# Moving the product keys behind the query blocks, and eleven of sixteen top-16 searches of each dense tile with them

## What is computed

```python
q = (tokens @ w_query).reshape(Ntok, PEER_HEADS, 2, PEER_DK)          # 8 heads x 2 halves x 128
s = jnp.einsum('nhpd,hpkd->nhpk', q, sub_keys)                        # 128 scores a list, 16 lists a token
s_top, i_top = lax.top_k(s, K)                                        # the 16 largest of each list
cand = (s_top[:, :, 0, :, None] + s_top[:, :, 1, None, :]).reshape(Ntok, PEER_HEADS, K * K)
best, pos = lax.top_k(cand, K)                                        # 16 experts a head
gate = jax.nn.softmax(best, axis=-1)
...
a = jax.nn.gelu(einsum('nd,nhkd->nhk', xb, expert_down[idx]));  y = einsum('nhk,nhkd->nd', gate * a, expert_up[idx])
```

## Time and profile before

| | |
|---|---|
| median of three runs | 1619.63 us |
| profiled execution, its own time | 1619.37 us |
| its span in the profile | 1617.6 us |
| PE busy | 1597.2 us (99%) |
| DVE busy | 1140.9 us (71%) |
| ACT busy | 665.7 us (41%) |
| POOL busy | 820.0 us (51%) |
| DMA, mean over the span | 263 GB/s |

### The profile page before, as it was taken

How to read it: one execution, slowest core, us unless ns; L and a number is a source line. 1 busy time by engine, 2 the same in 40 slices (tenths; PEclk the granted TensorE clock), 3 DMA queues, 4 the chain that set the end, 5 groups by cost and what they waited for, 6 DMA issues and landing times.

```text
span 1617.6 us, 25384 instructions
## 1 busy us (share of the span) xinstructions
PE 1597.2 (99%) x9227; PEld 1423.1 (88%) x9227; DVE 1140.9 (71%) x2214; ACT 665.7 (41%) x995; POOL 820.0 (51%) x523
## 2 busy tenths in 40 slices
PE   8999999999999999999999999999999999999998
PEld 6888888888889999999999999998888888888886
DVE  4155451351509999997999997339888888888887
ACT  5352442441534344434444544443333333333333
POOL 4463276423244989996877777856222222222220
PEclk9999999999999999999999999999999999999999
DMA  5332243313434999997999999949999999999992
GB/s 196 92 103 71 76 150 96 104 53 118 151 97 136 348 338 337 333 349 236 330 407 400 400 412 402 357 145 398 396 337 348 333 350 334 350 335 347 340 330 77
DMA packets 154442, 424.96 MB, mean 263 GB/s; under 512 B 15728, under 2 KB 65904, under 8 KB 154224
## 3 DMA queue, kind: packets, MB, share of 16 engines
q1 hardware_dynamic: 89088, 229.41, 41.5%
q0 software_dynamic: 41472, 151.01, 25.2%
q10 hardware_dynamic: 23792, 43.33, 7.0%
HBM read 379.88 MB, written 43.25 MB: 262 GB/s over the span
## 4 chain that ended last, share of the span: by engine, by line
PE 90%; DVE 4%; ACT 2%; POOL 2%; DMA 1%; issue 1%; DVEq 0%; SPq 0%; ACTq 0%
PE psum L1459 28%; PE psum L1461 27%; PE psum L1460 27%; PE psum L1748 4%; POOL w_low L457 1%; DMA hid_dram<-arena 1%; PE psum L1695 1%; ACT kept L547 1%; POOL arena L486 1%; DVE arena L1069 0%; ACT w_high L577 0%; PE psum L1582 0%; DMA kept<-x_in 0%; DVE hT_low L1041 0%; PE psum L1431 0%
## 5 line engine op out<-in xcount | busy, mean ns | idle before, releaser
L457 POOL TENSOR_TENSOR w_low<-kept,w_high 128x1024 fp32r<-128x1024 f32 x212 | 520.1, 2457 | 309.3 <-ACT w_high L577 307.5
L1459 PE MATMUL psum<-hT_high,w_high 128*128 128x352 f32 (+2 forms) x1408 | 483.9, 344 | 6.2 <-POOL w_low L457 6.1
L1461 PE MATMUL psum<-hT_high,w_low 128*128 128x352 f32 (+2 forms) x1408 | 477.1, 339 | 0.0
L1460 PE MATMUL psum<-hT_low,w_high 128*128 128x352 f32 (+2 forms) x1408 | 476.5, 338 | 0.0
L1459 PE MATMUL psum<-up_high,wgt_high 128*128 128x512 f32 x768 | 299.0, 389 | 0.0
L1460 PE MATMUL psum<-up_low,wgt_high 128*128 128x512 f32 x768 | 299.0, 389 | 0.0
L1461 PE MATMUL psum<-up_high,wgt_low 128*128 128x512 f32 x768 | 299.0, 389 | 0.0
L1459 PEld LDWEIGHTS psum<-hT_high,w_high 128*128 128x128 f32 x1408 | 265.3, 188 | 21.6 <-ACT arena L814 3.7
L577 ACT ACTIVATE w_high<-kept 128x1024 fp32r<-128x1024 f32 x212 | 223.7, 1056 | 128.1 <-PE psum L1461 91.2
L1460 PEld LDWEIGHTS psum<-hT_low,w_high 128*128 128x128 f32 x1408 | 265.1, 188 | 12.4 <-issue 0.5
L1461 PEld LDWEIGHTS psum<-hT_high,w_low 128*128 128x128 f32 x1408 | 264.8, 188 | 12.6
(11 more groups left out here) (251 smaller groups left out, 1956.4 us busy)
## 6 DMA issues: line engine op xcount, KB each, us to landing
kept<-down_in SPq DMA_DIRECT2D x128, 512.0 KB, 6.6
arena<-up_in SPq DMA_DIRECT2D x128, 512.0 KB, 5.7
kept<-front_w SPq DMA_DIRECT2D x92, 512.0 KB, 3.6
gate_dram<-arena ACTq DMA_DIRECT2D x40, 512.0 KB, 8.9
hid_dram<-arena ACTq DMA_DIRECT2D x112, 176.0 KB
arena<-hid_dram SPq DMA_DIRECT2D x112, 176.0 KB, 5.1
kept<-gate_dram SPq DMA_DIRECT2D x24, 640.0 KB, 8.3
arena<-gate_dram SPq DMA_DIRECT2D x8, 640.0 KB, 8.8
```

The costliest lines, as they stand in the source:

```text
L457: nc.gpsimd.tensor_tensor(lower, ring[:, p % RING, :], high.bitcast(F32), ALU.subtract).then_inc(low_ready, 1)
L1459: nc.tensor.matmul(out, lhs[0], rhs[0], start=first, stop=False)
L1460: nc.tensor.matmul(out, lhs[0], rhs[1], start=False, stop=False)
L1461: return nc.tensor.matmul(out, lhs[1], rhs[0], start=False, stop=last)
```

## The change

Each query block is followed by the key products of the list of the block before, for all tiles at once (`key_products`), and ACT copies them with one instruction into `score` (`key_out`). Two groups of sparse key products stay in front (`KS` = 2); the last dense products (n = 15) stand behind first product 0. DVE searches sparse list 8 + n as it comes, and behind it the same list of the three dense tiles for n = 0 to 6; list 15 and lists 0 to 2 of the dense tiles (n = 7 to 10, twelve lists) come after the sparse `choose` and its gates. Eleven of sixteen lists of a dense tile are thus searched outside its `choose`, into tiles of their own (`early_top`, `more_top`), and four copies bring them into `dense_k`. Each dense tile has two dots instead of three between the steps of its five other lists, so 18 a tile and `DOTS_A` = 54. `AHEAD` goes from 60 to 48, with all blocks that hang on it; the gathers of rows 5 and 6 move from i = 1 to i = 2, and `DOTS_END` goes from 14 to 26 rows, so that all 160 rows are still fetched.

```diff
-EXP_AT = (16, 32, 52)
-TURN_AT = (20, 40, 60)
+EXP_AT = (14, 26, 41)
+TURN_AT = (18, 33, 48)
...
-FIRST_EDGE = 44
+FIRST_EDGE = 32
...
-DOTS_SCORES = (3, 3, 3, 3)
+DOTS_SCORES = (2, 2, 2, 2)
+EARLY, MORE = 8, 3
...
-DOTS_END = (1,) * 14
+DOTS_END = (1,) * 26
...
-        KS = 4
+        KS = 2
+        KEYS = KS + 16
...
-                if i == FIRST_GATHER + 1:
+                if i == FIRST_GATHER + 2:
                     while k < RING_A:
                         if k == 5:
-                            pool.wait_ge(pk_done, KS + 4 * DT)
+                            pool.wait_ge(pk_done, KEYS)
                         down_row(k)
                         k += 1
-                while k < DOTS_A and i > FIRST_GATHER and (k - RING_A) * (AHEAD - 8 - FIRST_GATHER) < (i - FIRST_GATHER - 1) * (DOTS_A - RING_A):
+                while k < DOTS_A and i > FIRST_GATHER + 1 and (k - RING_A) * (AHEAD - 8 - FIRST_GATHER) < (i - FIRST_GATHER - 1) * (DOTS_A - RING_A):
...
+            def key_out(n):
+                j, tiles = (n + RAW) % 16, NT if n < 16 - RAW else DT
+                act.wait_ge(pk_done, KS + n + 1)
+                nc.scalar.activation(score[:, 0:tiles, j * NK:(j + 1) * NK],
+                                     psum[:, DB[n % 2], 0:tiles * NK].rearrange("p (t k) -> p t k", k=NK), ACT.Copy).then_inc(pk_out, 1)
...
             for n in range(16):
                 query_out(n)
...
+                if n:
+                    key_out(n - 1)
+                if n == 14:
                     act.wait_ge(best_ready, 1)
                     nc.scalar.activation(sparse_k.ebest, sparse_k.ebest, ACT.Exp).then_inc(e_ready, 1)
...
+            early_at(0)
+            key_out(15)
...
-            choose(score[:, ST, :], sparse_k, 0, (0, 0, 0, 0), (0, 0, 0, 0), 0, sparse_k.hk, 0, (2, KS))
...
+            dve.wait_ge(pk_out, KS)
+            top16(lists_of(ST, [place(sparse_k, j) for j in range(RAW)]), 0, none)
+            for n in range(EARLY):
+                dve.wait_ge(pk_out, KS + n + 1)
+                top16(lists_of(ST, [place(sparse_k, RAW + n)]) + (early_lists(n) if n < EARLY - 1 else []), 0, none)
+            choose(sparse_k, 0, none, 0, sparse_k.hk, 0)
             nc.vector.scalar_tensor_tensor(idx3.bitcast(U32), sparse_k.hk[:, 0, :], float(NK), sparse_k.hk[:, 1, :],
                                            ALU.mult, ALU.add).then_inc(idx_ready, 1)
             step(gates_of(sparse_k, gate3, 1))
+            for n in range(EARLY - 1, EARLY + MORE):
+                dve.wait_ge(pk_out, KS + n + 1)
+                top16(early_lists(n), 0, none)
...
             for n, t in enumerate(CHOSEN):
-                kd = choose(score[:, t, :], dense_k, kd, DOTS_SCORES, DOTS_CAND, DOTS_HOT, hk if n else hk_last, max(n - 1, 0))
+                for to, early, more in ((dense_k.top, early_top[t], more_top[t]),
+                                        (dense_k.topi.bitcast(U32), early_topi[t].bitcast(U32), more_topi[t].bitcast(U32))):
+                    step.put(nc.vector.tensor_copy(to[:, RAW:RAW + EARLY, :], early))
+                    step.put(nc.vector.tensor_copy(to[:, 0:MORE, :], more))
+                kd = top16(lists_of(t, [place(dense_k, j) for j in range(MORE, RAW)]), kd, DOTS_SCORES)
+                kd = choose(dense_k, kd, DOTS_CAND, DOTS_HOT, hk if n else hk_last, max(n - 1, 0))
...
             for n in range(16):
                 if n >= 4:
                     pe.wait_ge(qp_out, n - 3)
                 columns(68 + n, hT_half, SEQ if n < 16 - RAW else DN, 4 + n % 4)
...
+                if n:
+                    key_products(n - 1)
...
             for i in range(AHEAD):
+                if i == 1:
+                    key_products(15)
```

More of the change, by code:

```diff
@@ L212, in build @@
         hk = dense_k.hk
+        early_top, early_topi = ([at(kb + j, EARLY * TK, EARLY, TK) for kb in (205.5, 206.5, 99)] for j in (0, 0.5))
+        more_top, more_topi = ([at(92 + 0.375 * t + j, MORE * TK, MORE, TK) for t in range(DT)] for j in (0, 0.1875))
         esum = at(27.75, 16)
@@ L793, in _ @@
                 query_out(n)
-                if n == 8:
-                    sparse_key_out(2)
-                    sparse_key_out(3)
-            for c in range(4 * DT):
-                if c == 8:
-                    high(USED + 2)
-                act.wait_ge(pk_done, KS + c + 1)
-                g = KEY_ORDER[c // DT]
-                nc.scalar.activation(score[:, c % DT, g * 512:(g + 1) * 512], psum[:, PB[c], :], ACT.Copy)\
-                    .then_inc(pk_out, 1)
-                if c == 3:
+                if n:
+                    key_out(n - 1)
+                if n == 14:
                     act.wait_ge(best_ready, 1)
                     nc.scalar.activation(sparse_k.ebest, sparse_k.ebest, ACT.Exp).then_inc(e_ready, 1)
+            high(USED + 2)
             def early_at(i):
@@ L820, in early_tiles @@
                     early_at(i)
-            for i in range(4):
+            early_at(0)
+            key_out(15)
+            for i in range(1, 4):
                 early_at(i)
@@ L1193, in top16, with lists_of, choose @@
                 return k
-            def choose(scores, u, k, between_scores, between_cand, between_hot, hk, hk_free, copied=(None,)):
-                for part, groups in enumerate(copied):
-                    if groups is not None:
-                        dve.wait_ge(pk_out, groups)
-                    each = 16 // len(copied)
-                    k = top16([(scores[:, j * NK:(j + 1) * NK], u.top[:, j, :], u.topi[:, j, :].bitcast(U32))
-                               for j in range(part * each, (part + 1) * each)], k, between_scores)
+            def lists_of(t, places):
+                return [(score[:, t, j * NK:(j + 1) * NK], top, topi.bitcast(U32)) for j, top, topi in places]
+            def choose(u, k, between_cand, between_hot, hk, hk_free):
                 pairs = u.pairs.bitcast(BF16).rearrange("p (a r) -> p a r", r=2)
@@ L1263, in _, with place, early_lists @@
             step(nc.vector.tensor_copy(psum[:, 3, 0:P], at(205.5, P)))
-            choose(score[:, ST, :], sparse_k, 0, (0, 0, 0, 0), (0, 0, 0, 0), 0, sparse_k.hk, 0, (2, KS))
+            none = (0, 0, 0, 0)
+            def place(u, j):
+                return j, u.top[:, j, :], u.topi[:, j, :]
+            def early_lists(n):
+                j = (n + RAW) % 16
+                return [pair for t in range(DT) for pair in lists_of(
+                    t, [(j, early_top[t][:, n, :], early_topi[t][:, n, :]) if n < EARLY else
+                        (j, more_top[t][:, n - EARLY, :], more_topi[t][:, n - EARLY, :])])]
+            dve.wait_ge(pk_out, KS)
[4 more added lines that the diff above has]
+            choose(sparse_k, 0, none, 0, sparse_k.hk, 0)
             nc.vector.scalar_tensor_tensor(idx3.bitcast(U32), sparse_k.hk[:, 0, :], float(NK), sparse_k.hk[:, 1, :],
@@ L1716, in _, with key_products @@
             pe.wait_ge(ffns.high, 2)
+            def key_products(n):
+                j, bank = (n + RAW) % 16, DB[n % 2]
+                pe.wait_ge(qp_out, n + 1)
+                pe.wait_ge(pk_out, KS + n - 1 if n >= 2 else 1)
+                for t in range(NT if n < 16 - RAW else DT):
+                    ins = nc.tensor.matmul(psum[:, bank, t * NK:(t + 1) * NK],
+                                           qpT_s[:, j, :] if t == ST else qpT[:, j, t * P:(t + 1) * P],
+                                           keysT[:, j, :], start=True, stop=True)
+                ins.then_inc(pk_done, 1)
             for n in range(16):
@@ L1720, in _ @@
                 columns(68 + n, hT_half, SEQ if n < 16 - RAW else DN, 4 + n % 4)
-                if n == 8:
-                    pe.wait_ge(qp_out, 8)
-                    sparse_keys(2)
-                    pe.wait_ge(pk_out, 1)
-                    sparse_keys(3)
-            pe.wait_ge(pk_out, KS)
-            for c in range(4 * DT):
-                g, t = KEY_ORDER[c // DT], c % DT
-                pe.wait_ge(qp_out, max(c // DT * 4 + 4, {4: 13, 5: 14}.get(PB[c], 0)))
-                if c >= 4:
-                    pe.wait_ge(pk_out, KS + (c - 1 if c >= 10 else c - 3))
-                for hp in range(4 * g, 4 * g + 4):
-                    ins = nc.tensor.matmul(psum[:, PB[c], hp % 4 * NK:(hp % 4 + 1) * NK], qpT[:, hp, t * P:(t + 1) * P],
-                                           keysT[:, hp, :], start=True, stop=True)
-                ins.then_inc(pk_done, 1)
+                if n:
+                    key_products(n - 1)
             def first_product(i):
```

9 lines of the change are left out of this document (4 added, 5 removed).

## The result

The changed kernel takes **1633.56 us** (median of six runs, 1628.95 to 1638.40), the kernel before 1620.31 beside it. The ratio on record, which is not the quotient of these two medians, is 1.0076, with a 95% interval from 1.0058 to 1.0094. It is slower, by 13 us in the medians and 12.3 us by the ratio. The forecast was 1628.5. The range's upper end, 1633.0, lies 0.6 us under the raw median; the ratio applied to the 1619.63 us that the forecast started from gives 1631.9, inside the range. The profiled execution took 1631.19 us, 11.8 more than the profiled one of before.

The account below looks back on a forecast made before the run. PE was taken to bound the kernel, busy for 1597.2 of 1617.6 us. 1619.37 (profiled) + 7.4 (stall) + 1.5 (clock) = 1628.3, so 1628.5 us against the median; range 1622.5 to 1633.

Parts of the forecast that it names:

- PE, ACT: Up to block 0: PE starts it at 520.1, switching matmul kinds costs nothing, ACT's sparse exponential ends at 516.3.
- DVE to the first dot: DVE behind the exponential: gates, twelve lists of 16.1 us, `h_row`, copies, maxima; first dot done at 538.8, now 526.6.
- DVE had no slack after 481.82: DVE in the kernel before: no slack from the sparse tile's lists at 481.82 to the first dot at 525.44.
- POOL and the stall: At block 3: row 7 waits for its dot, low part ready at 543.5, PE waits 11.1 us, +7.4 us.
- rival A: At block 3: dots are in time, PE waits 0.6 us, time 1616.5 us; chance 0.07.
- C: At block 3: the stall is half, POOL or DVE order hiding some, 1620 to 1625 us; chance 0.09.
- The clock: PE behind the stall: a slow start after idling costs 1.5 us, between 0 and 3.
- Further on: From block 3 on: nothing won back, little lost, 0 to 2 us, taken as 0; last tile in time by 6 us.
- Rival B: Stall, then DVE's last tile misses 715, or ACT waits for best scores at `EXP_AT`: 1633.5 us; chance 0.12.
- The sentence on the copies: DVE's four copies of tiles 2 and 3 can each meet a POOL subtraction, making 0.9 us a tile too little.
- The range: Whole-kernel time: 1622.5 to 1633 us, meant to take in 8 of 10.

Follow-up runs that it names:

- e1: Changed kernel with the twelve searches behind the sparse gates left out, their outputs set to zero: 1626.04 us, ratio 1.0037 to the kernel before.
- e2: Changed kernel with sixty unread matmuls ahead of block 3 to keep PE busy in the stall: 1637.86 us, ratio 1.0104 to the kernel before.
- e6: Changed kernel with the old, longer calendar (gates behind block 59, 66 dots): 1629.02 us, ratio 1.0051 to the kernel before.
- e10: e6 with the sixty unread matmuls ahead of block 3: 1628.52 us, ratio 1.0058 to the kernel before.
- e12: e6 without the twelve searches behind the sparse gates, their outputs set to zero: 1617.80 us, ratio 0.9992 to the kernel before.
- e3: Changed kernel with rows 5 and 6 back behind block 1 instead of block 2: 1636.37 us, ratio 1.0103 to the kernel before.
- e8: e7 with gates behind block 55 instead of 59, 1.18 rows a block instead of 1.08: 1618.38 us, ratio 0.9991 to the kernel before.
- e5: Changed kernel with rows from 7 on started three blocks later and then denser: 1626.62 us, ratio 1.0043 to the kernel before.
- e7: Changed kernel with rows from 7 on three blocks later, gates behind block 59, 60 dots: 1615.62 us, ratio 0.9970 to the kernel before.
- e9: Kernel before, with rows 5 and 6 one block later and rows from 7 on three blocks later: 1620.28 us, ratio 0.9998.

## Why the prediction was right, and where not

- **PE, ACT:** block 0 at 519.98 (forecast 520.1), exponential done at 516.1 (516.3), no cost in changing between kinds of matmul. Right.
- **DVE to the first dot:** gates 516.1 (forecast 516.3), `h_row` at 533.17 (533.3), copies 0.5 us (0.9), first dot done at 538.3 (538.8). The twelve searches took 16.2 us (16.1). Right, and e1 shows that they are the cause. That DVE had no slack after 481.82 overlooks its wait of 1.6 us at 522.32, which changes no term.
- **POOL and the stall:** row 7 at 538.61 (538.9), low part ready at 543.2 (543.5), wait 10.9 us (11.1), +7.2 us (+7.4). Right; rival A and C are out.
- **The clock:** it fell, and cost 2.0 us in the trace (forecast 1.5, bounds 0 and 3). e2 shows that idleness is the cause.
- **"Further on" is the term that was mis-sized.** I set it at 0 with 2 at the most. In the profiled execution it was 2.6 us (11.8 less 9.2), and e6 against the changed kernel says 4 us by their ratios, whose intervals overlap. The time came out inside the range, or at its edge by the raw median, because the stall and the clock, the two terms of the forecast's 8.9 us, were each right to 0.5 us. The step compared POOL's own 3.8 us a block with PE's, and asked only whether DVE's last tile is in time, which it was (711.9, and PE asked at 717.4; forecast 709 and 715). It didn't compare dots with rows, though its own numbers held that: 18 dots in 57.7 us are 1.21 a block of 3.88, and the calendar issues 47 rows in 40 blocks, 1.18. By the trace the tiles took 58.5, 60.4 and 57 us, and the dots lay 3.22 us apart, which is 1.20 a block of 3.86. A row waits for the dot of seven rows before, a low part stands behind the row, and POOL, with 3.8 us of its own in 3.86, wins back little of what it loses at a tile's end. The kernel before had 1.14 rows a block to 1.16 dots: hardly more margin, but its row 7 went out 4.7 us behind its dot, where the changed kernel's went out on it, and no later gather waited. That this lead at the start counts beside the margin is argued from the traces and not tested.
- **Rival B** had the sign but not the place: no turn was missed. The sentence on the copies, by which each could meet a subtraction, came true for one of twelve (2.23 us at 654.56, the others 0.17 to 0.23), so the Trainium skill's sentence ("GPSIMD Engine Reference", Specifications) on the shared way to SBUF, weighed there, gives the direction and not the count. Other short operations met it more often, as the last section shows.
- **The range** had to hold this term's true width. Three of the six runs, 1635.9 to 1638.4, lie beyond its end.

## What to carry to other kernels

Before work is moved ahead of the first item of a chain that a ring of buffers ties together, compare the pace of producer and consumer per step, not only their due times, and ask how far ahead one of them starts: where the paces are nearly equal and there is no lead, each small delay stays. Ask of every queue behind which such a wait stands what else is in it; here two row fetches whose own dots began only 11 and 16 us later (rows 7 and 8) held the one subtraction that PE did need. And look for the calendar's room together with the work's place: the same key products and searches cost 0.8% with one placement of rows and turns and gained 0.3% with another, of which the placement alone gave 0.1%, not clear of noise.

## What was not expected of the hardware

- The clock's lower level set in during the idle time and went on for 4.4 us of work after it. Filling the idle time with matmuls that nobody reads kept it at 1.00 (e2, e10).
- Waits of PE much shorter than the stall lowered the clock too: behind 3.5 us it was 0.68 in the mean over the window from 560 to 570 us (e1), behind 1.9 us 0.83 (e12), and behind 1.8 us 0.83 from 645 to 655 us (e3). Not every such wait did: behind 1.9 us at 608.87 in e8 and 1.7 us at 647.20 in e2 it stayed at 1.00. What decides is not shown.
- Some short operations of DVE on SBUF that meet POOL's subtraction end with it. DVE's and POOL's timelines of the changed kernel:

```profile
567.70 2.89 DVE L1219 TENSOR_TENSOR arena<-arena 128x128 f32<-128x128 f32 x1
...
571.22 2.82 DVE L1229 TENSOR_SCALAR arena<-arena 128x128 bf16<-128x128 bf16 x1
574.08 0.29 DVE L1230 SCALAR_TENSOR_TENSOR arena<-arena 128x128 bf16<-128x128 bf16 x1
```

```profile
568.03 2.40 POOL L460 TENSOR_TENSOR w_low<-kept,w_high 128x1024 fp32r<-128x1024 f32 x1
...
571.57 2.41 POOL L460 TENSOR_TENSOR w_low<-kept,w_high 128x1024 fp32r<-128x1024 f32 x1
```

  Both long ones (L1219, L1229) end within 0.2 us of the subtraction beside them. They take 2.9 and 2.8 us; the same two lines took 0.29 and 0.20 us at 500.74 and 501.67, where POOL was idle. The operations between them fell into POOL's gather and kept their 0.3 us.
- A transfer can be what a kernel meets next when a stall goes: a store of 176 KB kept ACT waiting 5.76 us (e1), with the DMA engines at a share of 1.04.
- The same program's runs spread over 9 to 10 us in the changed kernel, e3 and e5, where gathers wait for dots. Of e7's twelve runs, without such waits, ten lie within 1.5 us, and the other two reach 1619.6. The kernel before has no such waits either, and 3 of its 29 runs beside e6 to e9 lie at 1625 against a median of 1619.7, so not all spread comes from them.
